# Attention steps of a hybrid decoder layer: transposes moved to the head of TensorE's step

## The chip, the cores and the metric

One NeuronCore of a Trainium2 chip. The metric is the device time of one execution in microseconds (us), lower is better. Durations come from one execution recorded by the hardware profiler.

## The reference, cut to what matters

One decoder layer on 1024 tokens of width 1024. The normalised input is projected to the operands of two attentions; their outputs are projected back, gated, merged and followed by a SwiGLU feed-forward block. The change touches the attention part alone:

```python
# A: sliding window of 128, 8 query heads over 2 key/value heads, rotary, a sink per head
p = exp(s - m);  p = p / (sum(p) + exp(sink - m));  o = p @ v
# B: causal, 8 heads, logits plus the cumulative log forget gate
s = q @ k.T * scale + cum[t] - cum[s];  p = softmax(s);  o = p @ v
```

## The kernel before, in words

Each engine runs its own hand-ordered list of instructions, and the lists are tied by semaphores. TensorE's list is written in `def _(pe)`. Every float32 product is made of three products of a high and a low part (`TERMS`).

After the first projections, TensorE runs 132 numbered **steps**, `gp` from -4 to 127 (lines 1557 to 1571). Steps 0 to 31 are attention A: token block `t` has the steps `2t` and `2t+1`, one per key/value head. Steps 32 to 127 are attention B: four pairs of heads with 24 steps each, starting at b = 32, 56, 80 and 104. Within a pair, steps b to b+7 hold the first half of the queries and b+8 to b+23 the second. A step holds up to four parts:

- `scores(r)` (line 1455; L1467 and L1473 for A, L1490 and L1494 for B): the scores of block row r. `s_step` gives the step: for A every even step from -4 to 26; for B's first pair b-6, b-4, b-4, b-3 (that is 26, 28, 28, 29) and b+1 to b+4; for the later pairs b-11, b-9, b-7, b-5 and b+1 to b+4. It waits until the banks of an earlier row have been read.
- `project(j, first, end)` (line 1412; L1436): a slice of a projection for a later pair. `fills` (line 272) deals 24 products out over the steps: 3 a step in steps 0 to 7; 6 a step in 12 to 15, 17 to 20 and 22 to 25; then 4 or 5 a step through most of B.
- `transpose_p(gp + 1)` (line 1497; L1509 for A, L1515 for B): up to four 128x128 transposes of the normalised probabilities of the next group. It waits for GpSimd to have normalised them (`norm_ok`), for VectorE to have read the bank it writes (`grp_lo`, two groups back), and for groups 0 and 1 for `proj_taken` 9 and 10, which VectorE gives when it is done with the rotary products of chunks 8 and 9.
- `times_v(gp)` (line 1519; L1542 and L1543): probabilities times values of the present group. It waits for the split of its transposed probabilities (`grp_lo`) and, in the first group of a unit, until the output bank has been read (`o_taken`).

The order in a step was: scores, projection, transposes of the next group, products of the present one.

The other engines walk the same numbers. ScalarE per step: `group_hi` (L798, high part of the transposes), `out_half` (L807, L808, L810, L812: half of an output, one step behind), the copies of a projection (L844), then `exps` (L782, L787) one step behind its scores. VectorE: `group_lo` (L1131), `out_add` (L1138, L1139, L1142), low parts of projections (L1199) or rotary products (L1059, L1062), `denominator` two steps behind its scores (L1125, L1126), then `score_stat` of this step's scores (L1093 to L1096 for A, L1112 for B). GpSimd: `normalise` (L657) two steps behind the scores, after that the splits of weights (L615, L617). SyncE loads weights ahead; neither its list nor any DMA is touched.

Of the kernel before, what the change touches and what calls it, by code (L numbers as in the profile page):

```python
# [39 lines left out]
def hybrid_layer(nc, x, c, positions, w_ada, b_ada, g_pre_mix, g_post_mix, w_in, b_f, sinks,  # L40
# [162 lines left out]
    NG = 2 * A_T + B_P * 3 * NTOK  # L203
# [18 lines left out]
    def banks(r):  # L222
        is_a, _, i = score_parts(r)
        if is_a:
            return [PS[:, 2 * (r % 2) + kv] for kv in range(2)]
        if i < 4:
            return [PS[:, 2 * (i % 2) + h] for h in range(2)]
        return [PS[:, 2 * h:2 * h + 2].rearrange("p a n -> p (a n)") for h in range(2)]

    def group_parts(gp):  # L230
        if gp < 2 * A_T:
            t, kv = gp // 2, gp % 2
            return True, t // NTOK, t % NTOK, kv, 0
        pb, k = divmod(gp - 2 * A_T, 3 * NTOK)
        return (False, pb, 0, k // 4, k % 4) if k < 8 else (False, pb, 1, (k - 8) // 8, (k - 8) % 8)

    def group_cols(gp):
        is_a, _, g, _, kb = group_parts(gp)
        if is_a:
            return 2 * P if g == 0 else NT  # L240
        return P * (4 * g + 4 - max(4 * g, kb))
# [89 lines left out]
    with ExitStack() as ctx:  # L331
# [238 lines left out]
        def _(pool):  # L570
# [76 lines left out]
            def normalise(r):  # L647

                is_a, _, i = score_parts(r)
                pool.wait_ge(rden_ok, r + 1)  # L650
                if is_a:
                    w = P if i == 0 else 2 * P
                    probs = [p_a[r % 3][:, hd, 0:w] for hd in range(4)]
                else:
                    probs = [s_row[i][:, h] for h in range(2)]
                for hd, pr in enumerate(probs):
                    ins = pool.tensor_scalar(pr, pr, rden[:, r % 4, hd:hd + 1], 1.0, ALU.mult, ALU.mult)  # L657
                ins.then_inc(norm_ok, 1)
# [695 lines left out]
        def _(pe):  # L1354
# [57 lines left out]
            def project(j, first, end):  # L1412

                n, ch = chunks[j]
                bank = chunk_bank(j)
                if first == 0:
                    pe.wait_ge(w_split, n + 1)
                    if j == 0:
                        pe.wait_ge(h_lo, 2 * KD)
                    elif j in (5, 6):  # L1420
                        pe.wait_ge(v_taken, 2 * NTOK)
                    elif j == 7:
                        pe.wait_ge(cum_taken, CH)
                    elif 8 <= j < 10:
                        pe.wait_ge(proj_taken, j - 3)
                    elif j == 10:
                        pe.wait_ge(proj_taken, 8)
                    elif j > 10 and chunk_bank(j) == 1:
                        pe.wait_ge(s_taken, A_T + NTOK * ((j - 14) // 4 + 1))
                    elif j > N_PROJ:  # L1430
                        pe.wait_ge(g_done, 1 if j == N_PROJ + 2 else 3)
                    elif j > 10:
                        pe.wait_ge(proj_taken, j - 1 if chunk_bank(j - 1) == 1 else j)
                for m in range(first, end):
                    k, (a, b) = m // 3, TERMS[m % 3]
                    ins = nc.tensor.matmul(PS[:, bank], w_hl[a][:, n % 2, k], act_hl[b][:, k, ch * NT:(ch + 1) * NT],  # L1436
                                           start=(m == 0), stop=(m == 3 * KD - 1))
                if end == 3 * KD:
                    ins.then_inc(proj_ready, 1)
# [57 lines left out]
            def transpose_p(gp):  # L1497
                is_a, pb, g, h, kb = group_parts(gp)
                if gp < 2:
                    pe.wait_ge(proj_taken, 9 + gp)  # L1500
                else:
                    pe.wait_ge(grp_lo, gp - 1)
                if is_a:
                    t = gp // 2
                    pe.wait_ge(norm_ok, t + 1)
                    for b in range(1 if g == 0 else 2):
                        for pl in range(2):
                            c = (2 * b + pl) * P
                            ins = nc.tensor.transpose(PS[:, 4 + gp % 2, c:c + P], p_a[t % 3][:, 2 * h + pl, b * P:(b + 1) * P],  # L1509
                                                      ident[:, :])  # L1510
                else:
                    pe.wait_ge(norm_ok, A_T + NTOK * pb + 4 * g + 4)
                    i0 = max(4 * g, kb)
                    for i in range(i0, 4 * g + 4):
                        ins = nc.tensor.transpose(PS[:, 4 + gp % 2, (i - i0) * P:(i - i0 + 1) * P],  # L1515
                                                  s_row[i][:, h, kb * P:(kb + 1) * P], ident[:, :])
                ins.then_inc(grp_ready, 1)

            def times_v(gp):
                is_a, pb, g, h, kb = group_parts(gp)  # L1520
                n = group_cols(gp)
                u = gp // 2 if is_a else A_T + 4 * pb + 2 * g + h
                if (h if is_a else kb) == 0:
                    if u == 0:
                        pe.wait_ge(proj_taken, 7)
                    else:
                        pe.wait_ge(o_taken, u)
                pe.wait_ge(grp_lo, gp + 1)
                p_hi, p_lo = pt_hl[gp % 3]
                if is_a:  # L1530
                    v = [va_hl[:, max(g - 1, 0) + b, h] for b in range(1 if g == 0 else 2)]
                    c0, m = 2 * P * h, 2 * P
                    first, last = True, True
                else:
                    v = [vb_hl[:, kb, 2 * pb + h]]
                    c0, m = NT - n, n
                    first, last = kb == 0, kb == 4 * g + 3
                for b, vv in enumerate(v):
                    both = vv.rearrange("p a d -> p (a d)")
                    cols = slice(b * m, (b + 1) * m)  # L1540
                    whole = PS[:, 6, c0:c0 + m]
                    nc.tensor.matmul(whole, both, p_hi[:, cols], start=first and b == 0, stop=False)  # L1542
                    ins = nc.tensor.matmul(whole, both, p_lo[:, cols], start=False, stop=last and b == len(v) - 1)  # L1543
                ins.then_inc(pv_done, 1)
# [10 lines left out]
            project(6, 0, 3 * KD)  # L1555
            project(7, 0, 3 * KD)
            for gp in range(-4, NG):
                if gp >= 0:
                    for r in range(N_S):
                        if s_step[r] == gp:  # L1560
                            scores(r)
                for j, first, end in mm_at[gp]:
                    project(j, first, end)
                if gp < 0:
                    for r in range(N_S):
                        if s_step[r] == gp:
                            scores(r)
                if 0 <= gp + 1 < NG:
                    transpose_p(gp + 1)
                if gp >= 0:  # L1570
                    times_v(gp)

# [194 lines left out]
```

## Time and profile before

| | |
|---|---|
| three runs, median | 1622.92 us (1621.88 to 1625.94) |
| profiled execution, its own time | 1621.15 us |
| its span, first to last instruction | 1619.4 us |
| TensorE busy | 1505.1 us, 93% of the span |
| VectorE, ScalarE, GpSimd busy | 586.6, 405.9, 640.2 us |
| mean granted TensorE clock | 0.98 of full speed |

The rows give the start of an instruction in us from the beginning of the span, its duration, engine, source line, operation, output and inputs, shape, how many were merged, and in brackets how long the engine sat idle just before it and whose work ended the idle time. TensorE's durations overlap, so its rate is read from start to start. The time outside the span is 1621.15 - 1619.4 = 1.75 us.

### The profile page before, as it was taken

Reading aid. Unit: us, or ns where it says so; the run is one execution under the profiler, and the core shown is the slowest. Engines: PE = TensorE matmul, PEld = TensorE weight load, DVE = VectorE, ACT = ScalarE, POOL = GpSimd, SP = SyncE. Lnnn points to the kernel's source line nnn. Section 1 sums busy time; section 2 is a strip of 40 time slices with the busy share of each in tenths; the row PEclk is TensorE's granted clock in tenths of the full one; section 3 lists DMA queues with packets and bytes.
Section 4 is the critical chain, followed back from the end, with each engine's and each line's share of the span. In section 5 each row is a group of like instructions: output and inputs, shape, how many; then the busy total and the mean of one; then the engine's idle time right before and its main releaser. Section 6 shows DMA issues by size and latency. Waiting matters only on the chain.

```text
span 1619.4 us, 18657 instructions
## 1 busy us (share of the span) xinstructions
PE 1505.1 (93%) x7273; PEld 1226.5 (76%) x7273; DVE 586.6 (36%) x913; ACT 405.9 (25%) x824; POOL 640.2 (40%) x515
## 2 busy tenths in 40 slices
PE   1599978899998999999999999999999999999998
PEld 1488746666766788888878788888888888788886
DVE  4683776655555565676655200000000000002002
ACT  2512046555545100001333200000000001434321
POOL 0501743323336355434202532333333233874860
PEclk9599999899999999999999999999999999999999
DMA  7500120102122464344332111111111121433531
GB/s 285 156 16 0 28 65 21 46 34 65 34 98 66 122 158 130 104 117 131 91 105 81 56 46 52 52 39 52 52 50 40 52 67 52 153 117 118 182 91 52
DMA packets 145396, 132.65 MB, mean 82 GB/s; under 512 B 13008, under 2 KB 125736, under 8 KB 144816
## 3 DMA queue, kind: packets, MB, share of 16 engines
q1 hardware_dynamic: 139824, 127.54, 25.3%
q10 hardware_dynamic: 5504, 4.20, 0.8%
q8 instruction: 44, 0.72, 0.2%
q14 instruction: 24, 0.20, 0.0%
HBM read 119.10 MB, written 12.62 MB: 81 GB/s over the span
## 4 chain that ended last, share of the span: by engine, by line
PE 79%; DVE 10%; ACT 4%; POOL 2%; issue 2%; DMA 1%; SPq 0%; DVEq 0%; ACTq 0%; POOLq 0%
PE PS L1358 66%; PE PS L1436 5%; PE PS L1490 2%; DVE s_row L1112 2%; PE PS L1515 1%; POOL s_row L657 1%; ACT p_a L782 1%; PE PS L1542 1%; DVE mx L1093 1%; PE PS L1543 1%; DMA xin<-in_x_dram 1%; PE PS L1369 1%; ACT pt_hi L798 1%; DVE rope_b L1062 1%; DVE act_lo L1025 1%
## 5 line engine op out<-in xcount | busy, mean ns | idle before, releaser
L1358 PE MATMUL PS<-act_hi,w_hi 128*128 128x512 f32 x928 | 362.6, 391 | 0.0
L1358 PE MATMUL PS<-act_lo,w_hi 128*128 128x512 f32 x928 | 361.8, 390 | 0.0
L1358 PE MATMUL PS<-act_hi,w_lo 128*128 128x512 f32 x928 | 361.6, 390 | 0.0
L617 POOL TENSOR_TENSOR w_lo<-wraw,w_hi 128x1024 fp32r<-128x1024 f32 x81 | 200.5, 2475 | 6.5
L1358 PEld LDWEIGHTS PS<-act_hi,w_lo 128*128 128x128 f32 x928 | 174.6, 188 | 36.7
L1358 PEld LDWEIGHTS PS<-act_hi,w_hi 128*128 128x128 f32 x928 | 174.5, 188 | 36.0
L1358 PEld LDWEIGHTS PS<-act_lo,w_hi 128*128 128x128 f32 x928 | 174.6, 188 | 35.9
L1334 DVE TENSOR_TENSOR act_ff<-PS,sl 128x512 f32 x40 | 27.7, 692 | 407.6 <-PE PS L1358 407.6
L615 POOL CAST w_hi<-wraw 128x1024 fp32r<-128x1024 f32 x81 | 87.1, 1075 | 187.9 <-PE PS L1358 112.7
L1358 PE MATMUL PS<-w_hi,ah_hi 128*128 128x512 f32 x352 | 137.0, 389 | 1.4 <-POOL w_lo L716 1.4
L1358 PE MATMUL PS<-w_hi,ah_lo 128*128 128x512 f32 x352 | 136.9, 389 | 0.0
L1358 PE MATMUL PS<-w_lo,ah_hi 128*128 128x512 f32 x352 | 136.9, 389 | 0.0
L923 ACT ACTIVATE sl<-PS 128x512 f32<-128x512 f32 x44 | 26.4, 600 | 430.8 <-PE PS L1358 430.8
L608 POOL TENSOR_TENSOR scratch<-ones 128x1 f32<-128x1 f32 x44 | 9.4, 214 | 301.0 <-PE PS L1358 295.3
L1131 DVE TENSOR_TENSOR pt_lo<-PS,pt_hi 128x512 fp32r<-128x512 f32 (+3 forms) x128 | 74.4, 581 | 117.4 <-ACT pt_hi L798 117.2
L716 POOL TENSOR_TENSOR w_lo<-w2raw,w_hi 128x1024 fp32r<-128x1024 f32 x44 | 106.3, 2416 | 6.6 <-ACT w_hi L948 6.5
L1436 PE MATMUL PS<-act_hi,w_hi 128*128 128x512 f32 x240 | 97.1, 405 | 3.6 <-DVE qb_lo L1199 1.9
L657 POOL TENSOR_SCALAR s_row<-s_row,rden 128x128 f32<-128x128 f32 (+7 forms) x64 | 46.9, 746 | 129.5 <-DVE rden L1126 129.3
L798 ACT ACTIVATE pt_hi<-PS 128x512 fp32r<-128x512 f32 (+3 forms) x128 | 65.3, 510 | 128.7 <-PE PS L1515 109.9
L1436 PE MATMUL PS<-act_lo,w_hi 128*128 128x512 f32 x240 | 95.7, 399 | 0.0
L1436 PE MATMUL PS<-act_hi,w_lo 128*128 128x512 f32 x240 | 95.0, 396 | 0.0
L713 POOL TENSOR_TENSOR ah_lo<-act_ff,ah_hi 128x512 fp32r<-128x512 f32 x44 | 57.0, 1295 | 63.3 <-ACT ah_hi L946 63.3
(223 smaller groups left out, 2522.7 us busy)
## 6 DMA issues: line engine op xcount, KB each, us to landing
wraw<-in_w_ffn_in_dram SPq DMA_DIRECT2D x44, 512.0 KB
w2raw<-in_w_ffn_out_dram SPq DMA_DIRECT2D x44, 512.0 KB, 3.6
adaraw<-in_w_ada_dram SPq DMA_DIRECT2D x32, 512.0 KB, 3.9
wraw<-in_w_in_dram SPq DMA_DIRECT2D x25, 512.0 KB
wada<-in_w_ada_dram SPq DMA_DIRECT2D x4, 2048.0 KB, 9.7
xin<-in_x_dram SPq DMA_DIRECT2D x8, 512.0 KB, 10.3
cs<-ncum_dram SPq DMA_DIRECT2D x4, 1024.0 KB, 4.8
woraw<-in_w_out_dram SPq DMA_DIRECT2D x8, 512.0 KB, 4.2
```

The source lines that it names most:

```text
L615: pool.tensor_copy(w_hl[0][:, slot], wraw[:, slot]).then_inc(w_hi_ok, 1)
L617: pool.tensor_tensor(w_hl[1][:, slot], wraw[:, slot], w_hl[0][:, slot].bitcast(F32), ALU.subtract)\
L657: ins = pool.tensor_scalar(pr, pr, rden[:, r % 4, hd:hd + 1], 1.0, ALU.mult, ALU.mult)
L713: pool.tensor_tensor(ah_hl[n][1][:, :], act_ff[:, m % FT, cols], ah_hl[n][0][:, :].bitcast(F32), ALU.subtract).then_inc(ah_split, 1)
L716: pool.tensor_tensor(w2_hl[n][1][:, :], w2raw[:, m % 2], w2_hl[n][0][:, :].bitcast(F32), ALU.subtract).then_inc(w2_split, 1)
L798: nc.scalar.activation(pt_hl[gp % 3][0][:, 0:n], PS[:, 4 + gp % 2, 0:n], ACT.Copy).then_inc(grp_hi, 1)
L1112: ins = nc.vector.tensor_tensor_reduce(out=s_row[i][:, h], in0=src[h][:, 0:w], in1=cs[:, h, 0:w], scale=-SM, scalar=BIG, op0=ALU.add, op1= ...
L1131: nc.vector.tensor_tensor(pt_hl[gp % 3][1][:, 0:n], PS[:, 4 + gp % 2, 0:n], pt_hl[gp % 3][0][:, 0:n].bitcast(F32), ALU.subtract).then_inc( ...
L1334: nc.vector.tensor_tensor(act_ff[:, bass.ds(it * 2 + ff, 1), ch * NT:(ch + 1) * NT] .rearrange("p a n -> p (a n)"), PS[:, 4 * (1 - ff) + 2 ...
L1358: ins = nc.tensor.matmul(out_ap, lhs[a], rhs[b], start=first and i == 0, stop=last and i == 2)
L1436: ins = nc.tensor.matmul(PS[:, bank], w_hl[a][:, n % 2, k], act_hl[b][:, k, ch * NT:(ch + 1) * NT], start=(m == 0), stop=(m == 3 * KD - 1))
L1490: nc.tensor.matmul(dst[h][:, c0:c0 + n], qb_hl[pb % 2][x][rows, i * P:(i + 1) * P], kb_hl[pb % 2][y][rows, c0:c0 + n], start=(e == 0), sto ...
```

## The change

TensorE's step is put in another order. For steps 0 to 126 the transposes of the next group now come first, then the scores, the projection slice and the products of the present group. In step -1 the transposes of group 0 stay where they were. The last step has none, as before. No instruction is added or taken away, and no other engine's list changes.

```diff
             for gp in range(-4, NG):
+                if gp >= 0 and gp + 1 < NG:
+                    transpose_p(gp + 1)
                 if gp >= 0:
                     for r in range(N_S):
                         if s_step[r] == gp:
...
                     for r in range(N_S):
                         if s_step[r] == gp:
                             scores(r)
-                if 0 <= gp + 1 < NG:
-                    transpose_p(gp + 1)
+                if gp == -1:
+                    transpose_p(0)
                 if gp >= 0:
                     times_v(gp)
```

## Rows read from the trace of the kernel before

**Rows 1.** Busy time in steps 0 to 127: length, PE, PEld, DVE, ACT, POOL, clock, DMA

```profile
208.00:537.00 329.00, 288.12 (x1744) 219.83 (x1745) 187.77 (x428) 172.84 (x457) 124.93 (x157) 0.97 0.17 53
```

**Rows 2.** Whom TensorE waited for, 195 to 540: us, times, longest

```profile
PE PS L1509 <- POOL p_a L657: 16.7, 12, 3.5
PE PS L1515 <- POOL s_row L657: 7.2, 5, 3.0
...
PE PS L1542 <- DVE ostage L1139: 4.5, 6, 1.9
...
PE PS L1542 <- DVE ostage L1142: 3.9, 8, 0.6
PE PS L1542 <- DVE pt_lo L1131: 3.2, 6, 1.0
```

**Rows 3.** Timeline, one period of attention A (block 5)

```profile
243.80 0.38 ACT L807 ACTIVATE ostage<-PS 64x256 f32<-64x256 f32 x1
...
245.96 1.84 POOL L657 TENSOR_SCALAR p_a<-p_a,rden 128x256 f32<-128x256 f32 x4 [4.74 <-DVE rden L1126]
...
247.94 0.63 PE L1509 MATMUL PS<-ident,p_a 128*128 128x128 f32 x4 [1.39 <-POOL p_a L657]
...
248.46 0.39 PE L1542 MATMUL PS<-pt_hi,va_hl 128*128 128x256 f32 x1
...
250.37 0.38 ACT L807 ACTIVATE ostage<-PS 64x256 f32<-64x256 f32 x1
```

**Rows 4.** Timeline, step 13; and in the chain, a projection slice of four

```profile
254.52 0.63 PE L1509 MATMUL PS<-ident,p_a 128*128 128x128 f32 x4 [0.33 <-POOL p_a L657]
...
255.34 0.28 PE L1543 MATMUL PS<-pt_lo,va_hl 128*128 128x256 f32 x1
...
256.07 0.38 ACT L807 ACTIVATE ostage<-PS 64x256 f32<-64x256 f32 x1
...
400.93 0.93 PE PS L1436 x4
```

**Rows 5.** Timeline, step 0

```profile
208.05 2.79 DVE L1062 TENSOR_TENSOR rope_b<-PS,cs 32x512 f32<-32x512 f32 x4
...
209.07 1.06 PE L1467 MATMUL PS<-maskb,identb 128*128 128x512 bf16 x2
...
211.64 0.59 PE L1436 MATMUL PS<-act_hi,w_hi 128*128 128x512 f32 x1
...
212.34 1.19 DVE L1093 TENSOR_REDUCE mx<-PS 128x4 f32<-128x1024 f32 x1
```

**Rows 6.** Timeline, steps 29 to 31

```profile
307.83 0.50 PE L1490 MATMUL PS<-kb_hi,qb_hi 64*128 64x512 f32 x2
...
308.85 0.61 PE L1509 MATMUL PS<-ident,p_a 128*128 128x128 f32 x4
...
312.57 3.38 POOL L657 TENSOR_SCALAR s_row<-s_row,rden 128x256 f32<-128x256 f32 x6 [3.25 <-DVE rden L1126]
```

**Rows 7.** Timeline of attention B, the pair with b = 56 and the ends of its neighbours

```profile
374.78 0.47 PE L1436 MATMUL PS<-act_hi,w_hi 128*128 128x512 f32 x1 [0.54 <-DVE qb_lo L1199]
...
397.42 0.63 PE L1515 MATMUL PS<-ident,s_row 128*128 128x128 f32 x4 [1.04 <-POOL s_row L657]
...
398.70 0.59 ACT L812 ACTIVATE ostage<-PS 64x512 f32<-64x512 f32 x1
...
399.44 0.69 DVE L1142 TENSOR_TENSOR ostage<-PS,ostage 64x512 f32<-64x512 f32 x1
...
400.19 0.50 PE L1542 MATMUL PS<-pt_hi,vb_hl 128*128 128x512 f32 x1 [0.56 <-DVE ostage L1142]
...
413.61 0.30 PE L1542 MATMUL PS<-pt_hi,vb_hl 128*128 128x128 f32 x1
...
415.88 0.50 PE L1542 MATMUL PS<-pt_hi,vb_hl 128*128 128x512 f32 x1 [0.42 <-DVE ostage L1142]
```

**Rows 8.** A window of TensorE alone: length, PE busy, granted clock, DMA

```profile
208.50:211.90 3.40, 3.28 (x17) 0.51 0.00 0
```

## The prediction

> **What bounds the kernel now.** I read the busy shares first (TensorE 93% of the span), then the busy times of the steps, TensorE's waits in them, and the timeline around each. The steps are one fifth of the span: 329 us in which TensorE is busy for 288 [rows 1]. So at most some 41 us could be won there, and any wait added lengthens the kernel unless TensorE waits anyway. Of the waits [rows 2], the two for GpSimd's normalised probabilities (16.7 + 7.2 = 23.9 us) stand before transposes; those that the new order could shorten stand before the products: 4.5 + 3.9 for the output bank, 3.2 for the split.
>
> The steps have two regimes. **In attention A the period is set by VectorE and ScalarE**, not TensorE: output half, output sum, denominator, maximum, exponentials, high part, next output half: 250.37 - 243.80 = 6.57 us [rows 3], and the other blocks keep it whether or not a step holds a projection slice. **In attention B TensorE sets the pace** but for a few places per pair [rows 7].
>
> **What moves.** No instruction is added, no DMA, no other engine's order. Between two products the same work stands as before, in another order; only what lies between a transpose and its neighbours differs. Two things follow. A transpose group comes earlier, so its split is ready long before its products. And it waits for normalisation *in front of* scores and projection, which used to run under that wait; all of TensorE stands behind it, and ScalarE and VectorE stand behind the scores and products.
>
> Costs of the blocks: after a wait, transposes take 248.46 - 247.94 = 0.52 us until the next block; a slice of four takes 0.93 [rows 4], so one of six 1.40; four products on 256 columns, behind a slice, some 0.65 until done (255.34 + 0.28 is 0.7 after their start; estimate).
>
> 1. **Step 0.** Transposes of group 1 need chunk 9's rotary products, done at 208.05 + 2.79 = 210.84 [rows 5]. They used to stand behind scores and slice, past that time; now TensorE waits for it, then transposes (0.45 at half clock), and the scores start at 211.35 instead of 209.07. They took 2.57 us at half clock, so they end near 213.9, and VectorE's maximum, which began at 212.34, begins 1.7 later; if the clock is back at 211.9 as before, about 0.7 later. Exponentials and the A period hang on it. I take +1.5, since TensorE idles in between.
>
> 2. **Odd steps of A with a slice.** Transposes of block t start at N (set by GpSimd), the output half at N + 2.43 (247.94 to 250.37, [rows 3]). New order: 0.52 + 1.40 + 0.65 + 0.05 = N + 2.62, so 0.2 late, and N of the next block follows the output half by 247.94 - 243.80 = 4.14, so the delay passes on. That holds in steps 17, 19, 23 and 25: +0.8. In step 13 the half began at 256.07, only 1.55 after N = 254.52 [rows 4]: +1.1. Step 15's block was short in the same way but its wait is already paid by step 13's delay. In steps 1 to 7 the slice is three: 0.52 + 0.70 + 0.65 + 0.05 = 1.9, under 2.43: nothing; its cover is ScalarE's exponentials. Together +1.9, bounds 0 (blocks shorter than I take) and +3.
>
> 3. **Even steps of A.** Scores come 0.45 later, by the transposes; the maximum that reads them has about 0.4 us of slack at full clock. Where the clock is at half, +0.2 in all.
>
> 4. **Step 29.** B's fourth row of scores ran from 307.83 to 308.85 under the wait for the last block of A [rows 6]. Now the transposes go first, at about 308.8, and the scores end at 310.4, 1.5 late. VectorE does their statistics before the next low part and output sum, the denominators behind them come later, and GpSimd's run that began at 312.57 and released step 31's transposes (3.38 us) starts some 1.2 late. +1.2, bounds 0 and +1.5. Steps 30 and 31 hold neither scores nor slice: unchanged.
>
> 5. **B, step b+7, four times.** Transposes of group b+8 start at 397.42, when GpSimd is done; that end is fixed by VectorE's and GpSimd's row 7, some 0.1 later than before as its scores come one transpose later. The slice of four that ran before now runs after: products at 397.5 + 0.52 + 0.93 = 398.95, done 0.45 later, then ScalarE 0.59 and VectorE 0.69 [rows 7] free the bank: the next products start near 400.9 instead of 400.19. +0.7 each, +2.8.
>
> 6. **B, step b+16, four times.** From the products at 413.61 to the next at 415.88 passes 2.27 us, since the output half stood behind the high part of transposes just made. That part is now long done: 0.4 + 0.6 + 0.7 + 0.15 = 1.85. -0.4 each, -1.6.
>
> 7. **B, the slice after the last step of a pair** (374.78, waiting 0.54 for a bank [rows 7]), three times, same reason: -0.45 each, -1.4. **Step 122** waits 0.5 for a split: -0.5. The other waits for a split (step b+6) come from the exponentials in front of it on ScalarE, not from the transposes: 0.
>
> Sum: 1.5 + 1.9 + 0.2 + 1.2 + 2.8 - 1.6 - 1.4 - 0.5 = **+4.1 us**, on the profiled 1621.15; the runs' median stands 1.8 above that, so 1622.9 + 4.1 = **1627.0**. A measurement of this kernel tells about 0.3%, 4.9 us, from no change; this is just inside.
>
> Term 2 hangs on the rate of a slice, 0.93 / 4 = 0.23 us a product [rows 4]. The Trainium skill (TensorE: Matmul & The Clock Gate, on the back-to-back issue gap) gives some 131 ns for a 512-column product in a stream of weight loads and products. By it six would take an estimated 0.79, the output half would still be covered, and the sum would be 2.2. The trace disagrees, and it decides.
>
> **The rivals.**
>
> *Half clock at the new gaps.* From 208.5 to 211.9 the granted clock was 0.51, so 1.2 GHz and not 2.4 [rows 8]; just before, TensorE had sat idle for 3.5 us, its longest wait [rows 2]. In step b+7 the idle time before the transposes grows from 1.04 by the slice, 0.93, to about 2.0 us. If each of the four places then gets 3.4 us at half clock in a stretch where TensorE sets the pace, each costs 1.7: 4.1 + 6.8 = +10.9, 1633.8, slower. It decides from two of the four (+7.5). For it: the fall near 208.5. Against it: 1.04 us of idle there bought no fall, and an A period idles 1.39 [rows 3] at full clock. The Trainium skill (same page, Part 1) calls the throttled state the default, released by activity; the row agrees. Chance 0.35, together with terms 1, 2 and 4 all at their upper bounds, which also lead past +4.9.
>
> *The waits before products were the real loss.* If the 11.6 us of such waits [rows 2] go, and GpSimd ends as much earlier because the whole ring turns faster, the kernel gains up to 11.6 and pays terms 1 and 5: -7, about 1616. For it: they are counted at 20 places. Against it: the A period does not contain them, and in B they end in other waits. Chance 0.10.
>
> *It does nothing measurable because the delays hide in one another*: step 0's delay gives slack to term 2, and step 29's run at GpSimd is met by slack: +1 to +2, 1624.5. This and the forecast share 0.55.
>
> **How the numbers follow.** Likeliest, 1627.0, own range 1623 to 1631. Past 1627.8 lie the first rival and the upper part of the forecast: slower 0.43. Faster by over 0.3%: 0.09. Within: 0.48. The range takes in some of the faster rival and the clock rival with three of four places: 1619.5 to 1633.
>
> **What would show it.** In the new profile: a wait of about 1.8 us of TensorE for VectorE's rotary products near 209; waits for GpSimd's probabilities up from 23.9 to about 35 us, waits for the split gone from all but b+6; the A period 6.8 us in steps 17 to 25 and 6.57 elsewhere; 2.0 us idle before group b+8; in B the second wait for the output bank of a pair down from 0.42 to under 0.2. The prediction is wrong if the A period stays at 6.57 throughout, if the granted clock of steps 32 to 127 falls, or if waits of about 1 us open before the scores.

## The result and the profile after

| | before | after |
|---|---|---|
| median of 16 runs each | 1622.73 us | 1629.3 us |
| lowest and highest | 1619.05 to 1626.54 | 1627.08 to 1635.36 |
| profiled execution | 1621.15 | 1629.08 |
| its span | 1619.4 | 1627.3 |
| mean granted TensorE clock | 0.98 | 0.975 |

The ratio is 1.0047, with a 95% interval of 1.0039 to 1.0055. That is 0.47% of 1622.7, some 7.6 us: slower, by more than the 0.3% that a measurement can tell. (The medians themselves lie 6.6 apart; the ratio pairs runs of the same rounds.) The forecast was +4.1 with 0.3% as its edge, so the time lies inside the stated range. The forecast had the right sign and a little over half the size, and it held slower by over 0.3%, which came, for a little less likely (0.43) than no change that can be told (0.48).

The first reading is the stretch of the steps, the answer to [rows 1]. The columns are length, busy TensorE, weight load, VectorE, ScalarE, GpSimd, granted clock, DMA.

```profile
208.00:545.00 337.00, 291.13 (x1748) 226.62 (x1748) 186.50 (x428) 175.18 (x459) 125.54 (x158) 0.95 0.16 51
```

The stretch is 8 us longer, and TensorE is busy for 3.0 of them with the same work, because its clock fell from 0.97 to 0.95. So there are two things to look for, idle time and half clock. The second reading is whom TensorE waited for, the answer to [rows 2] (us, times, longest):

```profile
PE PS L1509 <- POOL p_a L657: 20.3, 13, 3.5
PE PS L1515 <- POOL s_row L657: 10.4, 5, 2.5
PE PS L1542 <- DVE pt_lo L1131: 4.0, 7, 1.0
...
PE PS L1542 <- DVE ostage L1139: 2.9, 4, 1.1
...
PE PS L1509 <- DVE pt_lo L1131: 1.7, 1, 1.7
PE PS L1509 <- DVE rope_b L1062: 1.6, 1, 1.6
...
PE PS L1542 <- DVE ostage L1142: 0.3, 2, 0.2
```

The waits for GpSimd's probabilities rose from 23.9 to 30.7 us and two new ones stand before transposes, 1.7 and 1.6. Waits before products fell from 11.6 to 7.2: the output bank's 3.9 is down to 0.3, but the split's is up, not gone. Waits moved from the products to the transposes, and they grew by some 6 us on the way (30.7 + 1.7 + 1.6 + 7.2 for 23.9 + 11.6).

The third reading is the timeline, place by place: start, duration, instruction, and in brackets the idle time just before and what ended it. First step 0, the answer to [rows 5]:

```profile
211.06 0.69 PE L1509 MATMUL PS<-ident,p_a 128*128 128x128 f32 x2 [1.62 <-DVE rope_b L1062]
...
211.54 1.06 PE L1467 MATMUL PS<-maskb,identb 128*128 128x512 bf16 x2
...
214.22 1.22 DVE L1093 TENSOR_REDUCE mx<-PS 128x4 f32<-128x1024 f32 x1 [1.64 <-PE PS L1473]
```

Then steps 13 and 17, and step 29 with what follows it, the answers to [rows 4] and [rows 6]:

```profile
255.79 0.63 PE L1509 MATMUL PS<-ident,p_a 128*128 128x128 f32 x4 [1.69 <-DVE pt_lo L1131]
...
258.31 0.38 ACT L807 ACTIVATE ostage<-PS 64x256 f32<-64x256 f32 x1 [1.00 <-PE PS L1543]
...
269.18 0.63 PE L1509 MATMUL PS<-ident,p_a 128*128 128x128 f32 x4 [2.52 <-POOL p_a L657]
...
312.18 1.09 PE L1509 MATMUL PS<-ident,p_a 128*128 128x128 f32 x4 [1.70 <-POOL p_a L657]
...
315.21 0.69 DVE L1112 CUSTOM_DVE_ANT_0 s_row<-PS,cs 128x512 f32<-128x512 f32 x1 [2.64 <-PE PS L1494]
...
316.17 0.38 ACT L807 ACTIVATE ostage<-PS 64x256 f32<-64x256 f32 x1 [2.27 <-PE PS L1543]
...
318.18 3.38 POOL L657 TENSOR_SCALAR s_row<-s_row,rden 128x256 f32<-128x256 f32 x6 [5.45 <-DVE rden L1126]
```

And step b+7 of the second pair, the answer to [rows 7], beside the same place in the third:

```profile
402.51 0.63 PE L1515 MATMUL PS<-ident,s_row 128*128 128x128 f32 x4 [1.96 <-POOL s_row L657]
...
404.94 0.59 ACT L812 ACTIVATE ostage<-PS 64x512 f32<-64x512 f32 x1 [1.16 <-PE PS L1543]
...
407.04 0.40 PE L1542 MATMUL PS<-pt_hi,vb_hl 128*128 128x512 f32 x1
...
459.32 0.63 PE L1515 MATMUL PS<-ident,s_row 128*128 128x128 f32 x4 [1.97 <-POOL s_row L657]
...
461.09 0.59 ACT L812 ACTIVATE ostage<-PS 64x512 f32<-64x512 f32 x1 [0.50 <-PE PS L1543]
...
462.46 0.51 PE L1542 MATMUL PS<-pt_hi,vb_hl 128*128 128x512 f32 x1
```

Both have the same idle time in front. Yet from the transposes to the next group's products the one takes 407.04 - 402.51 = 4.53 us and the other 462.46 - 459.32 = 3.14. The stretches of half clock (same columns as the first fence) say why:

```profile
208.80:215.60 6.80, 5.18 (x22) 3.38 (x23) 5.02 (x9) 1.51 (x7) 4.37 (x6) 0.50 0.52 173
270.20:273.60 3.40, 3.40 (x13) 2.50 (x11) 1.10 (x2) 2.50 (x9) 0.00 (x0) 0.50 0.10 28
311.20:324.80 13.60, 9.12 (x37) 7.31 (x38) 6.03 (x18) 7.13 (x20) 4.91 (x10) 0.50 0.08 22
403.30:406.70 3.40, 3.40 (x13) 2.91 (x12) 1.65 (x3) 1.66 (x3) 0.00 (x0) 0.50 0.00 0
516.00:519.40 3.40, 3.40 (x13) 2.89 (x12) 2.08 (x3) 1.30 (x3) 3.32 (x3) 0.50 0.43 113
1389.80:1393.20 3.40, 3.40 (x9) 2.61 (x9) 0.00 (x0) 0.00 (x0) 3.40 (x3) 0.50 0.52 157
```

The rows at 270.2, 403.3 and 516.0 each follow a transpose group that TensorE had idled 2 to 2.5 us for. The kernel before has no half clock at these three places; in steps 26 to 32 it has two stretches of 6.8 us:

```profile
300.60:307.40 6.80, 5.96 (x30) 4.66 (x31) 4.20 (x16) 4.08 (x17) 4.65 (x6) 0.50 0.29 80
...
314.30:321.10 6.80, 5.00 (x17) 3.96 (x17) 1.69 (x4) 1.84 (x4) 1.66 (x3) 0.50 0.01 2
...
901.40:904.80 3.40, 3.40 (x10) 2.63 (x9) 1.98 (x3) 2.66 (x3) 3.37 (x3) 0.50 0.02 5
```

Around the change from A to B both kernels thus have 13.6 us of half clock, only at other places. Over all the steps it is 34.1 us after the change and 20.5 before: one stretch of 3.4 us more at step 0, one at step 17 and two at the steps b+7. In the kernel before one such stretch lies past the steps, near 901; after the change there was one near 1390 instead.

### The profile page after: what moved, and what is told of

The parts are those of the page before. It is cut to its first block, busy times and chain, and to the rows that moved or that the text cites. A ratio compares the mean times of both kernels' runs of the same rounds, so it can differ in the third digit from the quotient of the medians.

```text
span 1627.3 us, 18657 instructions
## 1 busy us (share of the span) xinstructions
PE 1507.3 (93%) x7273; PEld 1233.0 (76%) x7273; DVE 587.4 (36%) x913; ACT 407.8 (25%) x824; POOL 638.7 (39%) x515
## 4 chain that ended last, share of the span: by engine, by line
PE 81%; DVE 9%; ACT 3%; POOL 3%; issue 2%; DMA 1%; SPq 0%; DVEq 0%; ACTq 0%; POOLq 0%
PE PS L1358 66%; PE PS L1436 6%; PE PS L1490 2%; PE PS L1515 2%; POOL s_row L657 1%; DVE s_row L1112 1%; PE PS L1542 1%; PE PS L1543 1%; POOL p_a L657 1%; DMA xin<-in_x_dram 1%; PE PS L1369 1%; DVE rope_b L1062 1%; DVE act_lo L1025 1%; DVE ada_acc L1004 1%; PE PS L1509 1%
## 5 line engine op out<-in xcount | busy, mean ns | idle before, releaser
L716 POOL TENSOR_TENSOR w_lo<-w2raw,w_hi 128x1024 fp32r<-128x1024 f32 x44 | 106.3, 2416 | 7.9 <-ACT w_hi L948 7.8
```

The lines of the kernel that those rows point to most:

```text
L716: pool.tensor_tensor(w2_hl[n][1][:, :], w2raw[:, m % 2], w2_hl[n][0][:, :].bitcast(F32), ALU.subtract).then_inc(w2_split, 1)
```

## The experiments

Two theories stood at the start. **Places**: each place of the prediction costs or gives by the order alone, and the sum of the places is the whole. **Clock**: the longer idle time in front of transposes brings half clock, and that is the larger part. Unless said otherwise the edit is a condition `head` on the step: where it holds, the transposes stand at the head of the step, elsewhere in their old place.

```diff
-                if gp >= 0 and gp + 1 < NG:
+                head = ...
+                if 0 <= gp < NG - 1 and head:
                     transpose_p(gp + 1)
...
-                if gp == -1:
-                    transpose_p(0)
+                if gp == -1 or (0 <= gp < NG - 1 and not head):
+                    transpose_p(gp + 1)
```

Single profiles differ by up to 3 us past the steps, so I compare stages: from one output half to another, or to a transpose group, in each kernel's timeline, minus the same stage of before. "b+7" is from the transposes of group b+8 to the start of its products, one figure per pair, with (h) where the clock fell to half there. "To group 40" runs from the transposes of group 32 to those of group 40. "Rest of B" is the sum of the other stages up to the products of group 127. Left out are blocks 1 to 5 and the stage from block 14's output half to the transposes of group 32. They are the same as before to within 0.1 us, save for 0.9 in e_warm, 1.0 in e_noslice, 0.7 in e_not29, 0.5 in e_only29 and 0.2 in e_sfirst. Each row is one profiled execution.

| us more than before | step 0 | 13 | 17 | 19-25 | 29 | to group 40 | b+7 in the four pairs | rest of B |
|---|---|---|---|---|---|---|---|---|
| after | 1.13 | 0.96 | 0.77 | 0.39 | 2.15 | -0.52 | 0.38, 1.76h, 0.37, 1.74h | -2.44 |
| e_a_only | 1.13 | 0.96 | 0.78 | 0.41 | 2.14 | -0.73 | 0, 0, 0, 0 | 0.04 |
| e_b_only | 0 | 0.02 | 0.01 | 0.05 | -0.01 | 0.08 | 1.62h, 1.77h, 0.37, 1.77h | -2.43 |
| e_b_not7 | 0 | 0.71 | 0 | -0.01 | -0.12 | 0.01 | 0, 0, 0, 0 | -2.22 |
| e_warm | 1.14 | 0.97 | 1.23 | 0.23 | 0.46 | 0.66 | 0.37, 0.37, 0.36, 0.36 | -2.18 |
| e_not0 | 1.53 | 0.97 | 1.05 | 0.26 | 2.15 | 0.63 | 1.78h, 1.67h, 0.36, 0.37 | -2.32 |
| e_not01 | 0 | 0.96 | 1.68 | 0.51 | 2.14 | -0.51 | 0.36, 1.76h, 0.36, 1.67h | -2.32 |
| e_not29 | 1.12 | 0.97 | 1.29 | 0.26 | 0.49 | -0.54 | 0.37, 0.37, 1.76h, 0.37 | -2.29 |
| e_noslice | 1.12 | 0.55 | 0 | 0.13 | 1.95 | -0.21 | 0.36, 0.36, 1.76h, 0.36 | -2.39 |
| e_sfirst | 1.52 | 0.96 | 1.37 | 0.24 | 0.58 | -0.74 | 0.36, 0.37, 1.54h, 1.73h | -3.21 |
| e_only29 | 0 | 0.69 | 0 | 0 | 0.47 | -0.55 | 0, 0, 0, 0.74h | 0 |
| e_keep | 0 | 0 | 0 | 0 | -0.18 | -1.40 | 0, 0, 0, 0 | 0.05 |
| e_best | 0 | 0 | 0 | 0 | -0.17 | -1.18 | 0, 0, 0, 0 | -2.23 |

### The two attentions apart

`head = gp < 2 * A_T - 1` (steps 0 to 30 alone):

> The new order in steps 0 to 30 only (attention A), the old one from step 31 on. Theory of places (transposes at the head of a step cost what used to run under the wait for GpSimd: step 0, steps 13 to 25 with a slice, step 29): nearly all of the loss is here, +5 to +6 us against before, and in the profile TensorE's first transposes of attention B start about 5.6 us later than before. Rival (the loss is attention B's: longer gaps in step b+7 and the half clock they bring): +1 to +2 us only.

Measured: 1628.45 us (8 runs; before 1622.22), ratio 1.0038, 1.0026 to 1.0051, or +6.2.

`head = gp >= 2 * A_T - 1` (step 31 and all of B):

> The old order up to step 30, the new one from step 31 on (attention B). Theory of places: a pair gives back at steps b+16 and b+24 what it loses in step b+7, so -1 to +1 us where the granted clock stays at full, and 1 to 1.5 us more for each pair in which it falls to half behind the gap of step b+7. Rival (the loss is attention B's): +5 us or more.

Measured: 1625.56 (12 runs), ratio 1.0023, 1.0014 to 1.0032, or +3.3. Stage by stage the two parts are the whole: A's stages are the same to 0.02 us in e_a_only as in the changed kernel, and B's gains (rest of B) are the same to 0.01. The medians add to 9.6, where those of the changed kernel lie 6.6 apart. In the profiles the steps add to 4.7 + 3.4 = 8.1 us against 6.7, and the difference is one fall: three of the four pairs fell to half clock in e_b_only's profile where two did in the changed kernel's. The rival named before both runs, that the loss is B's alone (+5 us or more there, 1 to 2 in A), is out.

### Step b+7 alone, by order and by clock

`head = gp >= 2 * A_T - 1 and not gp in [step0(pb) + 7 for pb in range(B_P)]`:

> As the run before, but the four steps b+7 keep the old order too. Theory of places: only the gains are left (0.5 at each b+16, 0.2 to 0.4 at each b+24, 0.7 in step 122), -3 us against before, faster than both kernels, TensorE's idle time in front of group b+8 back at 1.0 us and no half clock there. Rival (the waits before products were the real loss, 11.6 us): -7 us or more. Rival (what is gained at one place is waited for at the next): 0.

Measured: 1621.31 (12 runs), ratio 0.9991, 0.9983 to 1.0: B without its four bad places is as fast as before or a little faster. Expected were -3 us. The steps gave -1.7: rest of B -2.2, less 0.7 at step 13, where the clock fell in the old order. Group b+8 starts after 1.06 us of idle time as in [rows 7], and no step of B behind group 40 runs at half clock:

```profile
398.24 0.63 PE L1515 MATMUL PS<-ident,s_row 128*128 128x128 f32 x4 [1.06 <-POOL s_row L657]
...
401.01 0.50 PE L1542 MATMUL PS<-pt_hi,vb_hl 128*128 128x512 f32 x1 [0.58 <-DVE ostage L1142]
```

For the clock, the new order everywhere, and in steps b+7 six products whose result nothing reads, put into the wait (a bank is free by then):

```diff
+                if gp in [step0(pb) + 7 for pb in range(B_P)]:
+                    pe.wait_ge(s_taken, A_T + NTOK * ((gp - 2 * A_T) // (3 * NTOK) + 1))
+                    for e in range(6):
+                        nc.tensor.matmul(PS[:, 2], act_hl[0][:, e, 0:P], act_hl[0][:, e, 0:NT], start=True, stop=True)
```

> The new order everywhere, and in each step b+7 six products of 512 columns into an unused bank ahead of the transposes (some 1.4 us of work that fits the idle 2.0 us; their results are not used). If the granted clock falls because TensorE idles in front of group b+8, it falls at none of the four places, and the time is 1 to 3 us below the new kernel's, +4 to +6 against before. If the gap has nothing to do with the falls, they still show in one or two pairs and the time is the new kernel's, +6.6; if the extra products delay the transposes, 0.5 more for each pair.

Measured: 1630.57 (6 runs), ratio 1.0044, 1.0028 to 1.006. The places themselves did change:

```profile
403.52 1.53 PE L1561 MATMUL PS<-act_hi 128*128 128x512 f32 x6
...
405.64 0.63 PE L1515 MATMUL PS<-ident,s_row 128*128 128x128 f32 x4 [0.60 <-POOL s_row L657]
...
408.78 0.50 PE L1542 MATMUL PS<-pt_hi,vb_hl 128*128 128x512 f32 x1
```

```profile
402.20:405.60 3.40, 2.35 (x11) 1.33 (x9) 0.68 (x3) 0.63 (x4) 3.23 (x4) 1.00 0.39 159
405.60:409.00 3.40, 3.34 (x19) 2.67 (x20) 1.63 (x3) 1.78 (x3) 0.00 (x0) 1.00 0.00 0
```

The transposes start when GpSimd ends, as before, but the clock stays at 2.4 GHz and the four places cost 0.36 to 0.37 us each. Over all kernels with the new order in step b+7 and nothing in the gap, the clock fell to half at 13 of 28 such places; with the gap filled at 0 of 4; with the old order at 1 of 24. **A fall costs 1.2 to 1.4 us on top of the 0.37 of the order** (1.54 to 1.78 in all), as pairs of the same kernel with and without one show. That the filling is what kept the clock up is likely but rests on four places: at 13 of 28, and if the places are independent, four without a fall come by chance about once in twelve (estimate). The total missed what was expected: it did not come down. In this profile the steps are 4.9 us longer than before (the row of the table with 0.9 for the blocks that it leaves out) against 6.7 in the changed kernel, but 2.8 us were lost past the steps and 2.6 ahead of them, where nothing was edited. The 2.8 are a longer wait near 1390 for GpSimd's split of a weight (`w_lo`, L716): 4.15 us, and 1.38 in the kernel before. With 6 runs the median can't tell such shifts from the gain, so that the steps' gain reaches the whole time is not shown.

### Attention A, place by place

`head = gp != 0`:

> The new kernel with the old order in step 0 alone. Theory of places: the wait of 1.6 us for the rotary products goes, the output half of block 0 starts where it did before, and what follows in attention A is 1.1 to 1.3 us earlier than in the new kernel. Rival (the delay is swallowed by slack further on, as steps 13 to 25 wait anyway): the first B transposes start at the new kernel's time.

Measured: 1633.32 (4 runs; before 1622.41), ratio 1.007, 1.0051 to 1.0088. Leaving step 0 alone made it worse, and the trace shows where it went. Step 1's transposes are now the first with a wait in front, and the clock falls there:

```profile
216.91 1.09 PE L1509 MATMUL PS<-ident,p_a 128*128 128x128 f32 x4 [2.96 <-POOL p_a L657]
```

```profile
216.30:219.60 3.30, 2.69 (x10) 2.44 (x11) 0.69 (x1) 1.77 (x8) 0.46 (x2) 0.50 0.24 71
```

So I kept both steps in the old order, `head = gp not in (0, 1)`:

> The new kernel with the old order in steps 0 and 1. With step 0 alone undone the start was no quicker: the clock fell in the gap before step 1's transposes and slice and products came behind them. If steps 0 and 1 are two places in a row of which either one costs, the start (first maximum to block 0's output half) is back at the 19.34 us of the kernel before, 1.1 less than the new kernel. Rival (the cost lies further on, in steps 2 to 7): still 1.1 longer.

Measured: 1629.91 (4 runs; before 1622.03), ratio 1.005, 1.0033 to 1.0068. The stage now costs 0.00, with the maximum at 212.43 (before 212.34, [rows 5]) and the next group at full clock:

```profile
212.43 1.19 DVE L1093 TENSOR_REDUCE mx<-PS 128x4 f32<-128x1024 f32 x1
...
216.28 0.63 PE L1509 MATMUL PS<-ident,p_a 128*128 128x128 f32 x4 [2.29 <-POOL p_a L657]
```

But the blocks behind it lost 0.9 more at step 17 (1.68 for 0.77), and the kernel is no faster: what the start gives, a fall later takes.

`head = gp not in (13, 15, 17, 19, 23, 25)`:

> The new kernel with the old order in steps 13, 15, 17, 19, 23 and 25, the odd ones that hold a slice of six products. Theory: output half of block t follows its transposes by 2.43 again and not by 2.6 to 2.65, and the period of A stays at 6.57: 2.0 us less in all than the new kernel by block 12 (which had 0.96 in step 13, 0.77 in step 17 and 0.1 to 0.2 in the others). Rival (ScalarE and VectorE set the period whatever TensorE does): nothing.

Measured: 1628.15 (5 runs; before 1622.41), ratio 1.0031, 1.0018 to 1.0044. Steps 17 to 25 cost 0.13 in place of 1.16, which with step 13 makes 1.4 us less for an expected 2.0; blocks 1 to 5, where a fall came at 230.4, took 0.8 more. Step 13's 0.55 stays although its order is the old one: the clock fell at 250.9, in front of it. e_b_not7 and e_only29, with the whole of step 13 as before, show 0.7 there, also with a fall (at 250.2 and 250.8). So at step 13 a fall costs about as much as the order, and the two don't add.

`head = gp != 29`:

> The new kernel with the old order in step 29 alone. Theory: the chain scores, statistics, output sum, denominators, GpSimd is what moves step 31's transposes, so these start 1.2 to 2.1 us earlier than in the new kernel. Rival: they wait for something else (the last block of A, or half clock that began earlier), and the change is under 0.5.

Measured: 1624.77 (10 runs; before 1622.41), ratio 1.002, 1.0008 to 1.0033: a step that is worth some 4 us of the 7.6, more than the 2.15 - 0.49 of its own stage. In the profiles 1.9 us of it lie in the steps and 1.5 past them, where this kernel has no half clock before 1619; how much of it repeats from run to run stays open. Its 0.49 is what half clock costs this stage in the old order, since the clock was at half from 308.3 to 315.1. `head = gp == 29`, the new order in this step alone:

> The old order everywhere, the new one in step 29 alone. In the new kernel the stretch from block 13's output half to block 14's was 2.15 us longer, with the granted clock at half from 311.2 on; in a kernel with the same order there and full clock it was 0.46 longer. If the order alone costs 0.5 and half clock the rest, this kernel is 0.5 later at block 14's output half when its stretch runs at full clock, up to 2 when a fall begins before step 29's scores. Time: +0.5 to +2 us, not to be told from no change.

Measured: 1624.95 (10 runs; before 1622.03), ratio 1.0013, 1.0002 to 1.0024. Its stage costs 0.47, not 2.15, since the clock was full from 308.8 on, before and after the transposes at 310.32:

```profile
302.00:308.80 6.80, 5.82 (x29) 4.51 (x30) 4.17 (x17) 4.03 (x16) 4.65 (x6) 0.50 0.24 68
309.00:312.00 3.00, 2.03 (x16) 1.28 (x16) 1.71 (x7) 3.00 (x10) 1.87 (x5) 1.00 0.29 85
```

e_warm has the new order, its transposes at full clock too, and costs 0.46. This parts the 2.15: 0.47 by the order, some 1.7 because the whole passage ran at half clock from 311.2 on. The two make more together than apart (0.47 and 0.49). With the scores in front of the transposes and half clock from 307.4 to 314.2 (e_sfirst, below) the stage costs only 0.58, so it is the scores behind the wait, done at half clock, that make the rest.

The table stops this stage at block 14's output half, and the order's price is not all in it. In e_only29 and e_warm the next stage, up to the transposes of group 32, is 0.49 us longer, in the changed kernel 0.06. From block 13's output half to group 32 the step costs 0.96 and 0.95 us with full clock around its transposes, and 2.21 in the changed kernel: 0.96 by the order and 1.25 by half clock. In e_only29 GpSimd's run that releases group 32 starts 0.96 us late as well (315.07, 8.90 us after block 13's output half; before, 312.57 and 7.94), in the changed kernel 2.21 us late.

### Another order: scores, transposes, slice, products

```diff
-                if gp >= 0 and gp + 1 < NG:
-                    transpose_p(gp + 1)
                 if gp >= 0:
                     for r in range(N_S):
                         if s_step[r] == gp:
                             scores(r)
+                if gp >= 0 and gp + 1 < NG:
+                    transpose_p(gp + 1)
                 for j, first, end in mm_at[gp]:
```

> Order scores, transposes, slice, products in every step: the transposes go ahead of the slice but not of the scores. Theory of places: step 0 costs nothing (the scores run under the wait for the rotary products) nor does step 29; the slices behind a wait (13 to 25, b+7) still cost: +2 to +4 us against before. Rival (any early transposes cost the same): +6.6.

Measured: 1627.93 (6 runs; before 1622.41), ratio 1.0034, 1.0021 to 1.0046. Step 0, expected to cost nothing, cost 1.52, with half clock from 215.2 to 222.0. Rest of B is the best of all, -3.21, and step 29 costs 0.58, but the slices stand behind the wait as they did, and steps 13, 17 and b+7 cost as much or more. In this profile the steps are 4.9 us longer than before, 1.8 less than in the changed kernel, so scores were the smaller part of the cover that was lost, as far as one profile with its own falls can tell.

### The clock, with the old order

If half clock costs, taking it from the kernel before should help. In the old order, 24 products whose result nothing reads stand in the idle time of steps 27, 30 and 31:

```diff
+                busy = {27: 8, 30: 5, 31: 11}.get(gp, 0)
+                if gp in (27, 31):
+                    pe.wait_ge(proj_taken, 14)
+                    for e in range(busy):
+                        nc.tensor.matmul(PS[:, 7], act_hl[0][:, e % KD, 0:P], act_hl[0][:, e % KD, 0:NT], start=True, stop=True)
...
+                if gp == 30:
+                    for e in range(busy):
+                        nc.tensor.matmul(PS[:, 7], act_hl[0][:, e % KD, 0:P], act_hl[0][:, e % KD, 0:NT], start=True, stop=True)
```

> The kernel before, order untouched, with 24 products of 512 columns whose results are not used, put where TensorE idles between the two attentions (8 ahead of step 27, 5 in step 30, 11 ahead of step 31's transposes). If a fall of the granted clock is brought by TensorE's idle time, the two falls at 300.6 and 314.3 (6.8 us each) do not occur, and the stretch from the first transposes of attention B to those of group 40 gets 1 to 2 us shorter. If the clock does not cost anything there, or the products only delay what follows, the stretch stays or grows.

Measured: 1622.39 (11 runs; before 1622.03), ratio 1.0001, 0.9991 to 1.0011. The two stretches of 6.8 us at half clock are gone:

```profile
300.20:307.00 6.80, 5.07 (x36) 3.28 (x34) 4.17 (x16) 4.63 (x17) 4.65 (x6) 1.00 0.27 70
314.00:320.80 6.80, 5.62 (x37) 4.08 (x37) 2.10 (x4) 1.85 (x4) 1.50 (x3) 1.00 0.07 19
1382.20:1385.60 3.40, 3.14 (x8) 2.50 (x9) 0.00 (x0) 0.00 (x0) 3.40 (x3) 0.51 0.42 154
```

and with them 1.5 us of the stages, 1.4 of them behind group 32, where TensorE sets the pace. The first stretch lay under VectorE's period and gave 0.18. The median shows none of it. In the profile the stage past the steps is 2.6 us longer: the wait for GpSimd's `w_lo` takes 4.10 us there for 1.38, and a stretch near 1382 stands in place of the one near 901. That what the steps give is waited for again at that place is a rival that these runs leave open.

Both together, e_b_not7's condition and these 24 products:

> The new order from step 31 on but for the steps b+7, with the same 24 products. The gains of both: 1.7 us from the places b+16 and step 122 and the like, 1 to 2 us from the clock: -2 to -4 us against before, faster than both kernels and than the run without the products. Rival: the falls come elsewhere instead, and it is no faster than that run.

Measured: 1620.37 (11 runs; before 1622.03), ratio 0.9989, 0.998 to 0.9998. Its steps are 3.4 us shorter than before, in the medians 1.7 arrive. It is the fastest of all, by less than the 0.3% that I hold to be worth telling.

## Why the prediction was right or wrong

Right were the sign, the places and most of the order's costs; wrong was the step "the rivals", which set half clock beside the forecast as another case, when it was most of this one. That the time fell inside the range is in part luck. Term by term, forecast against stages:

- **Step 0** (term 1): +1.5, measured 1.13. The scores came at 211.54 for a forecast 211.35 and the maximum 1.9 us later (1.7 within the stage), at half clock, as taken. Some 0.6 was won back in the block. Half clock lasted to 215.6 here where it had ended at 211.9, and no run has this order at full clock, so order and clock aren't parted in the 1.13.
- **Step 13** (term 2): +1.1, measured 0.96. The wait there is for the split two groups back [1.69 before 255.79], not for GpSimd, which I had not seen.
- **Steps 17 to 25** (term 2): 0.2 each, measured 0.77 for step 17, 0.24 for step 19 and 0.08 for steps 23 and 25. The forecast took a period of 6.57 us for every block; in the kernel before, those from block 5 on took 5.70 to 7.93. The slice's rate of 0.23 us a product holds in the trace: group 26's slice starts at 291.30 and its products at 292.76, (292.76 - 291.30) / 6 = 0.24, and the output half comes 2.52 after the transposes, against 2.43 in [rows 3]:

```profile
290.92 0.63 PE L1509 MATMUL PS<-ident,p_a 128*128 128x128 f32 x4 [1.49 <-POOL p_a L657]
291.30 0.47 PE L1436 MATMUL PS<-act_hi,w_hi 128*128 128x512 f32 x1
...
292.76 0.28 PE L1542 MATMUL PS<-pt_hi,va_hl 128*128 128x256 f32 x1
...
293.44 0.38 ACT L807 ACTIVATE ostage<-PS 64x256 f32<-64x256 f32 x1
```

  The 0.131 us a product of the Trainium skill (TensorE: Matmul & The Clock Gate, on the back-to-back issue gap) would, by an estimate, have hidden the slice in steps 17 to 25 wholly; no row here comes near it. (The sum of 2.2 that the prediction gives for it drops too much: by the same working step 13 would still be 0.52 + 0.79 + 0.65 + 0.05 - 1.55 = 0.46 late, and b+7 would cost less.) Step 17's excess of some 0.7 and step 19's are the clock: with the slice no longer in the wait, the idle time before its transposes is 2.52 where it was 0.60 in the kernel before, and half clock sets in at 270.2:

```profile
266.95 0.63 PE L1509 MATMUL PS<-ident,p_a 128*128 128x128 f32 x4 [0.60 <-POOL p_a L657]
```

  All seven kernels with the new order in step 17 idle 2.52 or 2.53 us there, and the clock fell in each of them within 266.7 to 271.6; the seven with the old order, before among them, idle 0.6 and have no fall there.

- **Even steps** (term 3): +0.2, measured nothing (blocks 1 to 5 within 0.02).
- **Step 29** (term 4): +1.2 for the transposes of group 32, measured 2.21, of which 0.96 by the order and 1.25 by half clock. The order's price was right; this is the single place that missed most. The rival had looked for new half clock in B only.
- **Group 32 to 40**: nothing forecast, measured -0.52. This is the clock too: 3.1 us of this stage ran at half clock where 5.0 had. Over all kernels the stage follows that time: 6.0 us at half clock gave +0.63 and +0.66, 4.6 us +0.01, 3.1 to 3.9 us -0.51 to -0.74, none -1.18 and -1.40.
- **Step b+7** (term 5): +0.7 each, measured 0.37 at full clock and 1.5 to 1.8 at half. The idle time grew to 1.96 as the rival said (1.04 + 0.93). The order's own price was half of what I took.
- **Step b+16, last slices, step 122** (terms 6 and 7): -1.6, -1.4 and -0.5, together -3.5; measured -2.4. From products to products step b+16 went from 2.27 to 1.74 us in all four pairs, -2.1, and step 122 gave -0.8, both more than forecast; the bank's waits fell to 0.3. The slice after a pair gave nothing net (-0.17 each up to the next pair's first products, then +0.22 in its first eight steps). The waits for a split rose by 0.8 us; those before scores (VectorE's statistics, `nm`) fell from 4.4 to 3.5, so where the rest of it went is not shown. I had taken waits that end in the next wait as gains, which the second rival's sentence "in B they end in other waits" already spoke against.

The sum by stages up to the products of group 127 is 6.7 us. Places by the order: 1.13 + 0.96 + 4 x 0.08 (steps 17 to 25) + 0.96 + 4 x 0.37 - 2.44 = +2.4. By half clock: 0.84 (steps 17 to 25) + 1.25 + 2.76 (b+7) - 0.52 = +4.3. The forecast's terms for the order were 1.7 us too high and the clock's share of 4.3 was missing, so +4.1 was as near as it is by two errors that partly cancel. Ahead of the steps the profile is 0.2 us longer and past them 1.0, which makes its 7.9.

The clock rival said two of the four places and +7.5; two of four fell in the profile and the runs gave +7.6, and in B it came near (3.4 for the two, measured 2.8). But the forecast that it built on held no new fall in steps 17 and 29 of A, where the clock cost 0.84 + 1.25 us.

Of what was to be seen in the profile: the wait near 209 came (1.62), GpSimd's waits rose (30.7 for a forecast 35), the 2.0 us before b+8 came, the second output-bank wait of a pair went to 0.2 or below. The split's waits did not go (4.0 + 1.7, was 3.2). And one of the stated signs of being wrong did show, a fall of the granted clock within steps 32 to 127: the mechanism was incomplete, though the time lay in the range.

The Trainium skill (same page, Part 1) calls the throttled state the default, released by activity. The trace agrees at the places that were filled: with the same wait and six products in it none of four fell, of 28 without them 13 did. Why it falls at one gap of 1.96 us and not at the next of 1.97 stays open here.

## What to carry to other kernels

- In an in-order list, the work that needs nothing late belongs in front of the wait, not behind it. The move took a slice of 0.93 us out from under GpSimd's wait; of the waits that it removed in attention B 2.4 us stayed won, others reappeared one instruction on.
- An idle gap of about 2 us on TensorE can cost twice, its length and then a stretch at half clock. Price both for every wait that grows, and in every stage, not in the one where it was first seen. Here 3.4 us of half clock cost 1.2 to 1.4 us where TensorE sets the pace. Under another engine's period it depended on the place: nothing near 243, where e_not01 without the fall takes as long, 0.7 at steps 13 and 17, and 1.25 up to group 32.
- Where whole spans scatter by 2 to 3 us, a change of a few us is read from stages between fixed instructions, each against the same stage of before.

## What the runs showed of the hardware that was not expected

Half clock at a gap is no fixed property of the kernel. At 28 like places with gaps of 1.96 or 1.97 us it came 13 times, at the gap of 2.52 us before step 17's transposes seven times of seven, and pairs of the same profile differ (403.3 and 516.0 in the changed kernel, not the first and third pair). Kernels that differ in one step also differ in falls far away: with step 0 in the old order it fell at 216.2, 349.4 and 407.4; with step 29 in the old order only at 458.5 in B. With one recorded execution each, whether the edit or the run moved them is not shown.

Past the steps, where all kernels run the same list, the stage up to the end was between 0.55 us shorter and 2.8 us longer than before. Two things go with it. One is the wait near 1385 for GpSimd's `w_lo` (L716), between 1.38 us (before) and 4.15 (e_warm). The other is a stretch at half clock near 900 in some profiles (901.4, 898.7, 909.1), near 1385 in others (1389.8, 1391.2, 1382.2), in three of them both, in three neither (e_a_only, e_not29, e_noslice, the three that are 0.5 us shorter). The change of that wait, and 1.7 us (estimate, half of 3.4) for each stretch more or less than the one of before, give all thirteen stages to within 0.6 us.

That bears on the runs of the changed kernel, ten of which lie between 1627.1 and 1629.7 and six between 1631.2 and 1635.4. Some profiles hold a stretch of 37.5 us at half clock near 38 us (before and after do, e_a_only and e_not29 don't), and the mean granted clock of a run seems to tell which: 0.975 or 0.976 for seven of the ten, 0.987 or 0.988 for the other three. A stretch of 3.4 us more takes 0.001 off this mean. Five of the six slower runs lie below their like, with 0.984 to 0.986 and once 0.970, as more falls would make it; the sixth, 1631.23 with 0.988, doesn't. Only one execution of each kernel was recorded, so that these two groups are such falls is a reading and was not shown.
